# Head 1's query product ahead of the first adds, its key ranking ahead of pair 2's dots and its expert numbers ahead of pair 3's dots

## The reference

```
q = (ht @ w_q).reshape(T, PEER_HEADS, 2, PEER_HALF)
sc = jnp.einsum('thpc,hpnc->thpn', q, sub_keys).astype(jnp.float32)
s1, i1 = lax.top_k(sc[:, :, 0], PEER_TOPK)
s2, i2 = lax.top_k(sc[:, :, 1], PEER_TOPK)
cand = (s1[..., :, None] + s2[..., None, :]).reshape(T, PEER_HEADS, PEER_TOPK * PEER_TOPK)
cand_id = (i1[..., :, None] * PEER_N_KEYS + i2[..., None, :]).reshape(T, PEER_HEADS, PEER_TOPK * PEER_TOPK)
top_s, pos = lax.top_k(cand, PEER_TOPK)
eid = jnp.take_along_axis(cand_id, pos, axis=-1)
g = jax.nn.softmax(top_s, axis=-1).astype(h.dtype)
...
    a = jnp.einsum('cd,chkd->chk', hc, u_tab[ec])
    w = gc * jax.nn.gelu(a)
    return jnp.einsum('chk,chkd->cd', w, v_tab[ec])
```

## Time and profile before

| | us |
|---|---|
| median of 3 runs | 905.53 (904.54 to 905.72) |
| the profiled execution, its own time | 903.55 |
| its span in the profile | 901.7 |
| PE matmul busy | 771.7 (86%) |
| DVE busy | 613.4 (68%) |
| ACT busy | 346.8 (38%) |
| POOL busy | 290.0 (32%) |
| granted TensorE clock, mean | 0.984 |

### The profile page before, as it was taken

One profiled execution on the slowest core, in us unless ns is written; L12 is line 12 of the kernel. 1 busy time (PEld: TensorE's weight loads), 2 busy tenths in 40 slices (PEclk: granted clock), 3 DMA queues, 4 the chain that ended last, 5 costly groups with the idle time before them and its releaser, 6 DMA issues.

```text
span 901.7 us, 8448 instructions
## 1 busy us (share of the span) xinstructions
PE 771.7 (86%) x2526; PEld 415.8 (46%) x2526; DVE 613.4 (68%) x1422; ACT 346.8 (38%) x1027; POOL 290.0 (32%) x280
## 2 busy tenths in 40 slices
PE   4999999999999999999997768787777777777777
PEld 2477877667556556565653323233322223222232
DVE  6788798954587967848758888758744444544445
ACT  3457688862144332423333242322422222222222
POOL 4000000000253544453537434453343334433320
PEclk9999999999999999999999998999999999999999
DMA  9977545679399999999999999999999999999995
GB/s 374 422 279 280 187 186 201 259 305 378 123 396 410 384 424 422 420 420 422 421 420 421 421 422 420 422 423 420 423 420 422 421 423 420 421 422 422 422 422 216
DMA packets 43956, 336.70 MB, mean 373 GB/s; under 512 B 4868, under 2 KB 4996, under 8 KB 7304
## 3 DMA queue, kind: packets, MB, share of 16 engines
q0 software_dynamic: 37296, 268.45, 71.9%
q1 hardware_dynamic: 6600, 67.72, 19.0%
q10 hardware_dynamic: 16, 0.00, 0.0%
HBM read 335.11 MB, written 1.05 MB: 373 GB/s over the span
## 4 chain that ended last, share of the span: by engine, by line
PE 45%; DMA 36%; DVE 11%; ACT 3%; issue 2%; another core or an unknown queue 1%; POOL 1%; SPq 0%; DVEq 0%; ACTq 0%
DMA ring<-in_peer_uv,eid 26%; PE ps_y L1645 19%; DMA rows<-in_peer_uv,eid 6%; PE bank L1613 4%; DMA extra<-in_peer_uv,eid 4%; PE bank L1579 3%; DVE ring L1040 2%; PE bank L1454 2%; PE bank L1456 2%; PE bank L1455 2%; PE bank L1594 2%; PE ps_y L1454 1%; PE ps_y L1418 1%; PE ps_y L1456 1%; PE ps_y L1455 1%
## 5 line engine op out<-in xcount | busy, mean ns | idle before, releaser
L1645 PE MATMUL ps_y<-ring,diag 128*128 128x512 f32 x568 | 268.2, 609 | 54.2 <-ACT diag L1329 54.2
L604 POOL DMA_INDIRECT ring<-in_peer_uv,eid x141 | 151.9, 1077 | 399.8 <-DVE eid L939 227.1
L1040 DVE CUSTOM_DVE_ANT_0 ring<-ring,gates 128x1024 f32<-128x1024 f32 x142 | 172.5, 1226 | 104.2 <-DMA ring<-in_peer_uv,eid 102.2
L1645 PEld LDWEIGHTS ps_y<-ring,diag 128*128 128x128 f32 x568 | 105.5, 192 | 200.1 <-issue 112.0
L1317 ACT ACTIVATE mask<-mask 128x2 f32<-128x2 f32 (+1 forms) x132 | 26.7, 203 | 373.8 <-DVE mask L1040 372.7
L1645 PE MATMUL ps_y<-rows,diag 128*128 128x512 f32 x136 | 68.8, 641 | 22.1 <-ACT diag L1329 17.6
L1329 ACT ACTIVATE diag<-ident,mask 128x128 f32<-128x128 f32 x256 | 87.3, 387 | 0.3
L1322 ACT ACTIVATE mask<-g_sb,mask 128x1 f32<-128x1 f32 x256 | 61.9, 287 | 4.3
L1040 DVE CUSTOM_DVE_ANT_0 rows<-rows,gates 128x1024 f32<-128x1024 f32 x34 | 41.5, 1227 | 31.1 <-DMA rows<-in_peer_uv,eid 28.6
L668 DVE TENSOR_TENSOR w_lo<-ring,w_hi 128x512 fp32r<-128x512 f32 x76 | 50.7, 684 | 10.5 <-PE bank L1456 8.8
L1136 ACT ACTIVATE w_hi<-ring 128x512 fp32r<-128x512 f32 x76 | 45.5, 626 | 22.7 <-PE bank L1456 22.4
(11 more groups left out here) (234 smaller groups left out, 1200.0 us busy)
## 6 DMA issues: line engine op xcount, KB each, us to landing
ring<-in_ada_t SPq DMA_DIRECT2D x11, 2048.0 KB, 9.8
ring<-in_in_t SPq DMA_DIRECT2D x10, 2048.0 KB, 10.0
ring<-in_up_t SPq DMA_DIRECT2D x2, 2048.0 KB, 8.8
ring<-in_out_t SPq DMA_DIRECT2D x2, 2048.0 KB, 13.9
kz<-in_peer_t SPq DMA_DIRECT2D x2, 2048.0 KB, 17.9
ring<-in_peer_uv,eid POOLq DMA_INDIRECT x141
x_sb<-in_x SPq DMA_DIRECT2D x2, 1024.0 KB, 12.2
ring<-in_ada_t SPq DMA_DIRECT2D x2, 1024.0 KB, 21.4
```

The costliest lines, as they stand in the source:

```text
L604: pool.indirect_dma_start(uv_row(n), None, peer_uv, bass.IndirectOffsetOnAxis(ap=eid[:, n:n + 1], axis=0)).then_inc(s_uv[name], 16)
L1040: dve.tensor_tensor_reduce(u_row(n), u_row(n), h2[:, n // P, :], 1.0, 0.0, ALU.mult, ALU.add, adot[:, at:at + 1]).then_inc(s_dot, 1)
L1645: ins = pe.matmul(ps_y[:, cut], diag[:, n % ND, :], v_row(n)[:, cut], start=first, stop=last)
```

## The change

Three numbers of the table `SLOT` change, and no instruction is added or removed:

```diff
-    "queries": ((None, 1, 3, 5, 13, 16, 25, 28), (7, 10, 19, 22, 31, 34, 37, 40)),
-    "keys": ((None, 2, 6, 18, 30), (42, 50, 58, 70)),
+    "queries": ((None, 0, 3, 5, 13, 16, 25, 28), (7, 10, 19, 22, 31, 34, 37, 40)),
+    "keys": ((None, 1, 6, 18, 30), (42, 50, 58, 70)),
...
-    "experts": ((None, 3, 10, 22, 34), (46, 54, 62, 74)),
+    "experts": ((None, 2, 10, 22, 34), (46, 54, 62, 74)),
```

## The result

| | before | changed |
|---|---|---|
| median of 5 runs, us | 905.24 (904.37 to 905.72) | 909.86 (908.82 to 910.97) |
| ratio to before | 1 | 1.0053 (95% interval 1.0038 to 1.0068) |
| the profiled execution: its own time, span | 903.55, 901.7 | 910.97, 909.2 |

The change makes the kernel 4.6 us slower; the interval is 3.4 to 6.2 us, and 5.4 had been forecast. The profiled execution of the changed kernel is the slowest of its five. In it the whole stage starts 1.36 us later: the query product begins at 259.62, behind the same instructions behind which pair 0's adds began at 258.26. So 1.36 is taken off wherever a time of after is set against one of before.

The account below looks back on a forecast made before the run. A DMA pipe full from about 310 us was taken as the bound, so earlier holes count. PE's chain lateness of 5.4 us (5.7 by holes) on 905.53 gave 910.9 us; forecast 909.4 to 912.0, 8-in-10 range 908.3 to 913.0.

Parts of the forecast that it names:

- The bound: DMA pipe full at 421 GB/s from about 310 us; only earlier holes, 3.4 us together, could be won.
- The copies on ACT: Head 1's two copies, queued ahead of pair 1's gelu, hold ACT until 263.65; the norm's root slips 4.23 us.
- Numbers 1.9 us later: Head 1's expert numbers on DVE: root 4.23 us late, less 2.30 for dots 3 moved behind them.
- Dots 3 behind the experts: DVE's dots of pair 3 follow head 1's numbers: PE's pair 3 adds 7.3 us late, pair 4's 5.37.
- the clock term: PE's pair 2 adds slowed after a 5.3 us pause: hidden, or 0.9 us on top, up to 911.8 us.
- the two cases of the earlier trace: PE pauses of 4.41 and 3.60 us, after which eight add records took 5.24 and 6.15 us instead of 3.44.
- Half clock: Rival, chance 0.09: pair 2's adds all at the lower clock, 6.9 us; pair 3's adds 1.6 us later, 912.5 us.
- The sum: PE, DVE and the gathers all 5.4 us later after row 21, with the pipe full from there: 910.9 us.
- The count by holes: Cross-check by DMA holes between 260 and 310 us: 9.1 us against 3.4 before, 5.7 more.
- The start and row 10: First DMA losses: 0.3 us at the start and about 1.5 as rows 10 and 11 are released later.
- rows 16 and 17: DMA holes while these gathers are late: 1.7 us at row 16, a new 2.8 at row 17.
- row 21: Gather freed by pair 5's adds, issued 5.4 us late at 299.0; its DMA hole about 1.8 us.

Follow-up runs that it names:

- e8_stall_late: Kernel before plus 28 chained small copies on ACT (6.5 us) in slot 80, nothing reordered: 904.61 us, ratio 0.9999.
- e5: Changed kernel, but PE's score product and ACT's two copies of head 1 stay in slot 1: 907.38 us, 1.0034 of before.
- e6: Kernel before with only head 1's query product in slot 0; scores, ACT's copies, keys and experts keep their places: 906.26 us, ratio 1.0016.
- e1: Kernel before with only head 1's query moved to slot 0, its scores and ACT's copies along with it: 909.16 us, ratio 1.0050.
- e3: Kernel before with only head 1's expert numbers moved ahead of pair 3's dots (slot 3 to 2): 908.40 us, ratio 1.0041.
- e7_stall_early: Kernel before plus 28 chained small copies on ACT in slot 0, ahead of pair 1's gelu, nothing reordered: 910.09 us, ratio 1.0058.
- e11: e6 plus the first half of head 3's query product in slot 4, ahead of pair 4's adds: 903.78 us, 0.9990 of before.
- e4: Kernel before with head 1's keys at slot 1 and experts at slot 2, query left at slot 1: 907.84 us, ratio 1.0037.
- e12: e3 plus the first half of head 3's query product in slot 3, ahead of pair 3's adds: 904.49 us, 0.9994 of before.

## Why the prediction was right, point by point

- *The bound.* Right. From 316 to 880 us both kernels move 421 GB/s, and e8_stall_late shows that a stall of 6.5 us on ACT there is free.
- *The copies on ACT, 4.23 us.* Right in kind, a little too large: the root was 3.98 us late. ACT's gelu starts 0.1 us before the `sc` copy has ended (264.92, with the copy from 264.64 for 0.38), and from there to the root it takes 3.33 us instead of 3.47. e5 against the changed kernel gives the wait 3.6 us by the rows and 2.0 by the medians, e6 against e1 2.9 by the medians.
- *Numbers 1.9 us later.* 1.70 measured. Taking dots 3 out gave its 2.3, and the root took more.
- *Dots 3 behind the experts: pair 3's adds 7.3 late, pair 4's 5.37.* Pair 3's adds started at 286.85 - 1.36 = 285.49, 0.4 later than worked out. That is the clock term: the price of pair 2's adds lay between the two cases of the earlier trace rows (5.91 us, against 5.24 and 6.15), and PE reached pair 3 0.6 us after DVE's dots would have let it (282.74 - 1.36 + 3.48 = 284.86). I had left it out of the sum and named it as what might come on top. Pair 5's adds were then 5.67 late for 5.37.
- *Half clock, the rival.* It did not come out in this kernel: 5.91 us, not 6.9, and 0.4 us of lateness at pair 3 for the rival's 1.6. The Trainium skill (TensorE: Matmul & The Clock Gate, Part 1) says that the clock is set by how busy the array has been. Here the trace agrees in kind, with 0.50 granted behind the pause of 5.02 us; that a pause by itself decides it, the runs do not bear out (last section). In e3 it came out nearly in full, 10.04 us for 16 records that take 6.9; eight of them at the lower clock would give 10.3.
- *The sum.* 5.4 forecast, 4.6 (3.4 to 6.2) measured by the medians. The chain in the profiled execution says 5.7, the holes 9.0 less 3.7, 5.3. Why the medians say some 0.8 us less than the one profiled execution, I cannot tell from one trace; the interval holds both.
- *The count by holes.* That it agrees so well, 9.1 forecast and 9.0 found, is in part luck. The start and row 10 were to cost 1.8 us and lack 2.2 (260 to 276), rows 16 and 17 were to cost 4.5 and lack 4.0 (282 to 292), row 21 was to cost 1.8 and 2.8 is missing behind it (292 to 316). The 1.0 us for ragged bytes and the 0.3 at the start had no row behind them, and no run shows them by themselves.
- *The point that the parts do not add.* e1 alone is +4.4 and e3 alone +3.6, together +4.6: query and experts delay the same adds. In e3 the pause stands ahead of pair 3, where nothing hides the fall of the clock (3.1 us). In e1 the clock falls too, at pair 2's adds (5.23 us after a pause of 2.01), but PE waits 1.74 us for DVE ahead of pair 4 all the same, and pair 5's adds are as late as the root, 3.98 us.

What stays open is the excess of e7_stall_early over its chain (5.2 measured, 3.7 by rows).

## What to carry to other kernels

A step moved earlier in a shared table is moved earlier on every engine's list; look on each for what now queues behind its waits, ACT's small copies above all. Before pricing a delay, ask whether the resource that sets the end has stock at that time: the same stall on ACT cost 5.2 us in slot 0 and nothing in slot 80. And fill a matrix engine's pause with work that is needed anyway: moving 1.8 us of it into a pause saved 3.7 us.

## What the runs showed of the hardware that I had not expected

The clock of TensorE falls after shorter pauses than the earlier trace rows show. These are pauses ahead of eight matmul records of adds, and what the records took from their start to the next instruction: 0.77 us, 3.54 (e11); 1.73, 3.53 (before, pair 4); 2.01, 5.23 (e1); 2.54, 5.10 (e6); 2.70, 5.24 (e4); 5.02, 5.91 (changed). For 16 records they are 1.12, 6.97 (e12) and 2.87, 10.04 (e3). But it does not follow from the pause alone: in e7_stall_early eight records come after 2.66 us and run at full speed, at a granted clock of 1.00 from 280 to 290:

```profile
286.85 3.70 PE L1653 MATMUL ps_y<-ring,diag 128*128 128x512 f32 x8 [2.66 <-ACT diag L1329]
290.39 1.05 PE L1621 MATMUL bank<-tT,v_sb 128*128 128x128 f32 x8
```

The kernel before has such a case as well, in time between the two cases of the earlier trace rows; its eight records take 3.54 us after a pause of 3.33:

```profile
499.88 1.98 PE L1645 MATMUL ps_y<-ring,diag 128*128 128x512 f32 x4 [3.33 <-ACT diag L1329]
...
503.42 1.88 PE L1645 MATMUL ps_y<-spare,diag 128*128 128x512 f32 x4
```

Against it stands e1_query_only, with the shortest pause of this list that cost something:

```profile
274.13 3.11 PE L1645 MATMUL ps_y<-gates,diag 128*128 128x512 f32 x4 [2.01 <-ACT diag L1329]
...
279.36 1.05 PE L1613 MATMUL bank<-tT,v_sb 128*128 128x128 f32 x8
```

What decides the cost of a pause besides its length stays open.
